# Last layer's output projection with the tokens on the partitions, and its layer norm along rows

## What is computed

```
def _layer_norm(x, g, b):
    mu = jnp.mean(xf, axis=-1, keepdims=True)
    var = jnp.mean(jnp.square(xf - mu), axis=-1, keepdims=True)
    return (xf - mu) * lax.rsqrt(var + LN_EPS) * g + b
...
    mixed = jnp.concatenate([y_conv, y_attn, y_lru], axis=-1) @ w_out
    return _layer_norm(DEEPNORM_ALPHA * h + mixed, ln_post_g, ln_post_b)
...
    return h[:, N_META:]
```

## Time and profile before

| | us |
|---|---|
| runs, median of 3 | 2905.97 (2905.51 to 2907.51) |
| profiled execution, its own time | 2904.78 |
| its span in the profile | 2902.7 |
| TensorE busy | 2791.1 (96%) |
| DVE busy | 1843.0 (63%) |
| ACT busy | 1434.4 (49%) |
| mean granted TensorE clock | 0.977 of 2.4 GHz |

### The profile page before, as it was taken

The page is one execution under the profiler, slowest core; times in us unless marked ns, Lnnn a source line. Parts: engine busy times, 40 slices in busy tenths (PEclk is TensorE's granted clock), DMA queues, the critical chain, the costliest instruction groups (busy, mean ns, idle before and its releaser), DMA issues.

```text
span 2902.7 us, 46087 instructions
## 1 busy us (share of the span) xinstructions
PE 2791.1 (96%) x17361; PEld 2502.7 (86%) x17361; DVE 1843.0 (63%) x2388; ACT 1434.4 (49%) x2149; POOL 150.3 (5%) x146
## 2 busy tenths in 40 slices
PE   7999999999999999999999999999989899999897
PEld 6888888888878878888888888888988889988896
DVE  6656565656565565656565656657887756787754
ACT  4545454545454444444444444445646744646733
POOL 0000000000000010101010100000000000000001
PEclk8999999999999899999999999999999999999998
DMA  6655555555556446555656565555533345543342
GB/s 191 181 177 181 177 181 177 181 177 181 177 159 190 144 148 181 178 180 177 180 177 180 177 181 161 177 187 177 160 121 120 124 138 169 158 131 118 123 141 70
DMA packets 472592, 472.28 MB, mean 163 GB/s; under 512 B 17800, under 2 KB 468000, under 8 KB 472480
## 3 DMA queue, kind: packets, MB, share of 16 engines
q1 hardware_dynamic: 469312, 470.01, 52.7%
q10 hardware_dynamic: 3184, 0.93, 0.1%
HBM read 468.76 MB, written 2.13 MB: 162 GB/s over the span
## 4 chain that ended last, share of the span: by engine, by line
PE 83%; DVE 10%; ACT 5%; issue 2%; ACTq 0%; DMA 0%; POOL 0%; SPq 0%; DVEq 0%
PE proj L1171 32%; PE proj L1173 16%; PE proj L1186 8%; PE proj L1340 5%; PE proj L1341 5%; PE proj L1342 5%; PE proj L1188 4%; DVE w_both L1929 2%; DVE scratch L2083 2%; ACT w_both L824 1%; PE ps_s L1248 1%; PE ps_s L1231 1%; DVE w_both L1625 1%; PE ps_t L1238 1%; PE ps_s L1249 0%
## 5 line engine op out<-in xcount | busy, mean ns | idle before, releaser
L1171 PE MATMUL proj<-operand,w_both 128*128 128x512 f32 x4096 | 1465.5, 402 | 17.1 <-DVE operand L1699 10.0
L1625 DVE TENSOR_TENSOR w_both<-w_raw,w_both 128x1024 fp32r<-128x1024 f32 x644 | 810.2, 1261 | 720.6 <-ACT w_both L638 720.0
L1173 PE MATMUL proj<-operand,w_both 128*128 128x256 f32 x4096 | 1151.4, 281 | 0.0
L638 ACT ACTIVATE w_both<-w_raw 128x1024 fp32r<-128x1024 f32 x644 | 682.4, 1060 | 930.4 <-PE proj L1173 703.0
L1171 PEld LDWEIGHTS proj<-operand,w_both 128*128 128x128 f32 x4096 | 773.3, 189 | 205.6 <-issue 14.7
L1173 PEld LDWEIGHTS proj<-operand,w_both 128*128 128x128 f32 x4096 | 777.7, 190 | 0.8
L1340 PE MATMUL proj<-operand,w_both 128*128 128x272 f32 (+1 forms) x1796 | 533.2, 297 | 23.4 <-DVE operand L2162 23.2
L1341 PE MATMUL proj<-operand,w_both 128*128 128x272 f32 (+1 forms) x1796 | 525.2, 292 | 0.0
L1342 PE MATMUL proj<-operand,w_both 128*128 128x272 f32 (+1 forms) x1796 | 523.9, 292 | 0.0
L1929 DVE TENSOR_TENSOR w_both<-w_raw,w_both 128x1024 fp32r<-128x1024 f32 x226 | 281.8, 1253 | 207.3 <-ACT w_both L824 206.7
L1340 PEld LDWEIGHTS proj<-operand,w_both 128*128 128x128 f32 x1796 | 344.6, 192 | 30.0 <-DVE operand L2162 24.5
(11 more groups left out here) (335 smaller groups left out, 1933.5 us busy)
## 6 DMA issues: line engine op xcount, KB each, us to landing
w_raw<-in_a_w_in_dram SPq DMA_DIRECT2D x256, 512.0 KB, 3.7
w_raw<-in_w_in_dram SPq DMA_DIRECT2D x160, 512.0 KB, 3.6
w_raw<-in_b_w_in_dram SPq DMA_DIRECT2D x128, 512.0 KB, 3.7
w_raw<-in_kv_w_dram SPq DMA_DIRECT2D x128, 512.0 KB, 3.9
w_raw<-in_a_w_out_dram SPq DMA_DIRECT2D x64, 512.0 KB, 4.4
w_raw<-in_b_w_out_dram SPq DMA_DIRECT2D x64, 512.0 KB, 4.4
w_raw<-in_w_out_dram SPq DMA_DIRECT2D x64, 512.0 KB, 3.4
scratch<-in_a_rel_bias_dram SPq DMA_DIRECT2D x16, 256.0 KB, 3.8
```

The costliest lines, as they stand in the source:

```text
L638: act.activation(w_hi[:, s], w_raw[:, s], ACT.Copy).then_inc(hi_ready, 1)
L1171: pe.matmul(proj[:, 2 * bank + t, :], w_hi[:, s, kk, cols], rhs[:, k, :], start=first and k == 0, stop=False)
L1173: m = pe.matmul(proj[:, 2 * bank + t, 0:S], w_lo[:, s, kk, cols], rhs[:, k, 0:S], start=False, stop=last and end)
L1625: dve.tensor_tensor(w_lo[:, s], w_raw[:, s], w_hi[:, s].bitcast(F32), ALU.subtract).then_inc(pieces_split, 1)
```

## The change

The last layer alone is changed. Its output projection holds 128 tokens of y in the array and streams the weights: a piece is 16 matmuls, eight of 512 columns (`w_hi` and `w_lo` side by side) and eight of 256 columns, and the meta tokens are left out. The residual is turned by TensorE in four chunks into the banks of `ps_t` and `ps_s`, and copied back by ACT, scaled by 1.414, into `x_res`, now with tokens on the partitions. DVE adds both halves of a bank to it. For each unit ACT sums the 256 features of each token and then the squares about that unit's own mean; DVE merges the eight means and sums of squares at the end. Gain and shift rows, copied to all partitions (two transfers of 1 MB), are loaded during the projection; two DVE instructions for each of the eight blocks give the output. The matmuls with ones, the last turning, and POOL's part fall away.

```diff
+        gain_row, shift_row = scratch[:, 0:D], scratch[:, D:2 * D]
+        out_rows = scratch[:, 2 * D:4 * D].rearrange("p (t n) -> p t n", t=2)
+        def token_rows(first, count):
+            return x_res[:, first:first + count, META:T].rearrange("p k (t f) -> p t k f", t=2)
...
                 for j in range(2, OUT_N):
+                    if l + 1 == DEPTH and j == 4:
+                        sp.wait_ge(y_split, 7 * DEPTH)
+                        for n, dst in ((0, gain_row), (1, shift_row)):
+                            row = io["layer_rows"][l, n * KT:(n + 1) * KT, :].rearrange("(a r) p -> a (r p)", a=1)
+                            sp.dma_start(dst, row.to_broadcast([P, D])).then_inc(final_rows_in, 16)
                     for chunk in (1, 2, 3, 0):
                         load_piece(rows_of(w_out, chunk, j * UNIT_N))
...
+            for t in range(2):
+                for c in range(4):
+                    columns = slice(c * 512, (c + 1) * 512)
+                    sp.wait_ge(out_ready, 4 * t + c + 1)
+                    sp.dma_start(io["out"][0, t * P:(t + 1) * P, columns], out_rows[:, t, columns]).then_inc(out_stored, 16)
...
+                def copy_residual(c):
+                    act.wait_ge(residual_turned, c + 1)
+                    act.activation(token_rows(4 * c, 4), (ps_t, ps_s)[c % 2].rearrange("p t (k f) -> p t k f", f=P), ACT.Copy, scale=ALPHA)\
+                       .then_inc(residual_copied, 1)
+
+                def chunk_stats(j):
+                    z = token_rows(2 * j, 2)
+                    act.wait_ge(proj_free, o0 + O_OUT + j + 3)
+                    if j:
+                        act.wait_ge(chunk_squared, j)
+                    for t in range(2):
+                        m = act.activation(conv_sq[:, t, 0:UNIT_N].rearrange("p (k f) -> p k f", k=2), z[:, t], ACT.Copy,
+                                           accum_out=chunk_sum[:, t, j:j + 1])
+                    m.then_inc(chunk_summed, 1)
+                    act.wait_ge(chunk_mean_ready, j + 1)
+                    for t in range(2):
+                        m = act.activation(conv_sq[:, t, 0:UNIT_N].rearrange("p (k f) -> p k f", k=2), z[:, t], ACT.Square,
+                                           bias=chunk_mean[:, t, j:j + 1], accum_out=chunk_m2[:, t, j:j + 1])
+                    m.then_inc(chunk_squared, 1)
...
+                    else:
+                        if j >= 1:
+                            chunk_stats(j - 1)
+                        if j < 4:
+                            copy_residual(j)
+                        if j == OUT_N - 1:
+                            chunk_stats(j)
+            act.wait_ge(row_var_ready, 1)
+            act.activation(row_stats[:, 4, :], row_stats[:, 3, :], ACT.Sqrt).then_inc(row_root_ready, 1)
...
+                def token_pieces(output, groups):
...
+                        s = next_split()
+                        for kk in range(PK):
+                            k = group * PK + kk
+                            for t in range(2):
+                                tokens = slice(META + t * P, META + (t + 1) * P)
+                                pe.matmul(proj[:, bank + t, :], y[0][:, k, tokens], w_both[:, s, kk].rearrange("p a n -> p (a n)"),
+                                          start=k == 0, stop=False)
+                                m = pe.matmul(proj[:, bank + t, 0:UNIT_N], y[1][:, k, tokens], w_hi[:, s, kk, :],
+                                              start=False, stop=k == KT - 1)
...
+                def turn_residual(c):
+                    pe.wait_ge(pw_taken, 2 * l + 1 + c % 2)
+                    if c >= 2:
+                        pe.wait_ge(residual_copied, c - 1)
+                    for kk in range(4):
+                        for t in range(2):
+                            m = pe.transpose((ps_t, ps_s)[c % 2][:, t, kk * P:(kk + 1) * P],
+                                             x_res[:, 4 * c + kk, META + t * P:META + (t + 1) * P], ident)
+                    m.then_inc(residual_turned, 1)
...
+                def mixed_rows(j):
...
+                    dve.wait_ge(residual_copied, j // 2 + 1)
+                    step(dve.tensor_tensor(z, z, halves[:, 0], ALU.add))
+                    dve.tensor_tensor(z, z, halves[:, 1], ALU.add).then_inc(proj_free, 1)
...
+            dve.wait_ge(final_rows_in, 32)
+            for t in range(2):
+                for c in range(4):
...
+                    step(dve.scalar_tensor_tensor(rows, z, minus_mean[:, t:t + 1],
+                                                  gain_row[:, columns].rearrange("p (k f) -> p k f", f=P), ALU.add, ALU.mult))
+                    dve.scalar_tensor_tensor(out_rows[:, t, columns], out_rows[:, t, columns], row_rstd[:, t:t + 1],
+                                             shift_row[:, columns], ALU.mult, ALU.add).then_inc(out_ready, 1)
```

More of the change, by code:

```diff
@@ L296, in build_program @@
         conv_sq = two.take(2, T)
+        chunk_sum, chunk_mean, chunk_m2, chunk_off = (two.take(2, OUT_N) for _ in range(4))
+        row_stats = two.take(8, 2)
         rows_in = scratch[:, temp0:temp0 + 2 * DEPTH * P].rearrange("p (a l b) -> p a l b", a=2, l=DEPTH)
@@ L2276, in _ @@
[L2276 to L2284 removed]
+                    if l + 1 < DEPTH:
+                        mixed(j)
+                    else:
+                        if j >= 1:
+                            negate_mean(j - 1)
+                        mixed_rows(j)
+                        if j == OUT_N - 1:
+                            negate_mean(j)
```

139 lines of the change are left out of this document (58 added, 81 removed).

## The result

| | before | after |
|---|---|---|
| runs of both on one chip, median | 2906.74 (2905.51 to 2912.44) | 2882.01 (2879.87 to 2884.94) |
| profiled execution, its own time | 2904.78 | 2881.66 |
| its span | 2902.7 | 2879.9 |

The ratio is 0.9912 (95% interval 0.9895 to 0.9929), which is 2880.4 (2875.5 to 2885.3) on the forecast's base of 2905.97.

The account below looks back on a forecast made before the run. TensorE, 96% busy, was taken to bound the kernel outside the end, a serial chain across engines. The end's 18.1 us plus the projection's 2.0 gave 20.1 us less, 2886 against the median; range 2882 to 2890.5.

Parts of the forecast that it names:

- The end: From TensorE's last matmul to the span's end: 19.4 us instead of 37.5, 18.1 less; gain bounds 15.5 to 18.6.
- the pair of output instructions: DVE's two 512-element instructions per output block at the end: 1.33 us a pair, eight pairs 10.7 us.
- The table load: ACT's load for the square root, behind the squares at the end: 1.3 us, without the skill page's 1.38 us drain.
- rival 2: At the end, the table switch before the root costs more than its load, at most 1.11 us: 2887.1; 5%.
- The projection: Last layer's output projection on TensorE: shorter pieces save 5.7 us, turns cost 3.6, net 2.0 less.
- the piece: Eight matmul pairs at 0.352 us in the projection: 2.82 us, 0.21 less a piece, counted for 27 pieces, 5.7 us.
- The turns: Four groups of eight turned f32 blocks on TensorE's path in the projection: 0.9 us a group, 3.6 us more.
- What I cost at nothing: During the projection, ACT's added instructions, DVE's unit of 6.6 of 11.3 us and SP's two 1 MB copies: no TensorE delay.
- Rivals 1, 3 and 4: 1: turns cost 3.6, pieces gain 0 to 2, 2889.5 to 2891.5, 8%. 3: ACT delays `hi`, TensorE stops each unit, 2906, 2%.
- rival 4: SP's two copies run slowly, delaying weight loads; TensorE stops for their time less 3 + 12 us; slower, 2923 at 40 GB/s; 2%.
- 18.1 + 2.0 = 20.1 us less: Whole kernel: savings at the end and in the projection added, giving 2884.7 for the profiled execution and 2886 against the median.
- its first form, 2882.5 to 2888.5: Whole kernel: the forecast's own range by the terms' bounds, widened to 2882 to 2890.5 to hold 8 in 10.

Follow-up runs that it names:

- immediates: Changed kernel with constants in place of each token's mean and reciprocal root in the sixteen output instructions, so the norm is left out; 2883.23 us (one run).
- turns_in_wait: Changed kernel with the first two groups of residual turns moved ahead of TensorE's last wait for y; 2879.00 us, ratio 0.9897 to the kernel before.
- rows_6mb: Changed kernel with four more 1 MB copies behind the two for gain and shift, and DVE waiting for them before the output; 2888.34 us (one run).
- after_narrow: Changed kernel with scratch at its old 18640 columns, the norm's small tensors at unused columns inside it; 2888.32 us, ratio 0.9929 to the kernel before.
- before_wide: Kernel before with only scratch widened by 40 columns, to 18680; 2899.25 us, ratio 0.9973 (0.9961 to 0.9985) to the kernel before.
- after_20: Changed kernel with its small tensors inside the old scratch columns, and scratch at 18660, so consts stand 80 bytes further; 2872.64 us, ratio 0.9880 to the kernel before.

## Why the forecast held in its parts and missed as a whole

- **The end** was forecast at 19.4 and is 20.2. All links up to the output are within 0.15 us. The mis-sized term is the pair of output instructions: 1.45 instead of 1.33 us, eight times 0.12 = 1.0. I had taken 692 ns from rows 10, an instruction whose scalar is a constant; immediates gives back 1.33 and an end of 19.2.
- **The table load** costs 1.28, the root follows at once, and rival 2 is out. The drain of 1.38 us that the Trainium skill gives (ScalarE: Activation LUTs, What ACT_TABLE_LOAD costs) doesn't show here: the load starts at 2863.42, some 20 ns after the last read of squares, and the root at 2864.71. To take the load away is worth 0.6 here.
- **The projection** was forecast at -2.0 and is -2.9. Ahead of the last wait for y it is -0.2 as counted: a shorter piece there only lengthens the wait. Behind it, the term is the piece: 2.795 us, 0.235 less than before instead of 0.21, 26 times 0.025 = 0.7 of the 0.9 that are missing there. I took the pair of rows 5 at 0.352, and in the projection it is 0.3495. The turns are 0.9 each, as said (0.92 in after, 0.87 in turns_in_wait). The formula of the Trainium skill (TensorE: Matmul & The Clock Gate, Back-to-back issue gap) is given there for an isolated matmul, which the prediction didn't say; an estimate from it is 2.60 for a piece, and the trace has 0.2 more.
- **What I cost at nothing** was nothing: ACT's five instructions, DVE's unit, the two copies. They landed 6.7 to 8.8 us after their issue, and TensorE has no wait in units 2 to 7. Rivals 1, 3 and 4 are out; but rows_6mb shows that rival 4 left out the clock (the stop cost twice its length) and had the margin some 2.6 us too wide.
- **The agreement of the sum** behind the copy, 20.2 against 20.1, is in part luck: the end gained 0.8 less than forecast and the projection 0.9 more, and the two misses cancel.
- **The step that failed** is the sum itself, "18.1 + 2.0 = 20.1 us less", which puts the stretch ahead of the changed part at nothing without a reason. The instructions there stay, but the addresses behind `scratch` don't. With the addresses held (after_narrow) the gain is 20.6, which is inside the range; the 40 columns are worth about 6 us by TensorE's pace and 6 to 8 by the runs, and 6 us below 2886 is outside of it. That the miss was only 1.6 us is within the noise of the runs; the effect of the columns is not, since before_wide's interval leaves out 1.
- **The range** had no bound for this. Nor is its first form, 2882.5 to 2888.5, what the bounds of the terms give: the ends of the two terms put together are 2883.5 and 2894.1.

## What to carry to other kernels

A change that makes a tensor larger moves every tensor behind it. Compare the pace of an untouched loop (matmuls in a long window, start to start) before the gain is put down to the edit, and hold the addresses for one run. Such a loop can have two paces, so look at it in several stretches and in more than one execution. Where a long serial end can be rebuilt for another layout, price it link by link with instructions of the same form, operands included: constant or column, PSUM or SBUF. Idle time of TensorE ahead of its last wait is room for work that it has later, as long as no buffer behind it then comes late (1.0 of 1.8 us were lost so here), and it pays more in the executions in which the clock would have fallen.

## What the hardware showed that I had not expected

- A stream of pairs of a 512- and a 256-column matmul runs at 346.7 or at 353.3 ns a pair, at full granted clock in both cases. It keeps its pace until other matmuls cut it; in 480 pairs without a cut one build had either value.
- What share of the stretches gets which pace goes with the place of a tensor that the pairs don't read: 352.2, 350.2, 348.9 and 350.0 ns on average for `consts` 0, 32, 80 and 160 bytes further. That was up to 14 us for the kernel (after_20 beside after_narrow, by the ratios).
- A wait of TensorE of 2.39 us was followed by some 3.4 us at a granted clock of 0.50 in after and by none in after_again; one of 2.75 us (rows_6mb) was followed by some 7 us and cost 5.8, twice its length.
- DVE's SCALAR_TENSOR_TENSOR of 512 elements takes 60 ns more (752 against 692) when its scalar comes from a column of SBUF.
- While two copies of 1 MB that read one row for all 128 partitions ran beside the weights, the queue moved 354 to 403 GB/s, and TensorE had no wait.
